# An encoder layer on one core: query norms moved into the softmax's exponential, and a bias table laid out backwards

## What is computed

```python
xn = rmsnorm(h, g_pre_mix)
proj = xn @ w_in                       # qa, ka, va, qb, kb, vb, gate_a, gate_b
qb = axial_rope(rmsnorm(qb.reshape(B, S, GQA_Q_HEADS, HEAD_DIM), g_q))    # 8 heads of 128
kb = axial_rope(rmsnorm(kb.reshape(B, S, GQA_KV_HEADS, HEAD_DIM), g_k))   # 2 heads
ya = neighbourhood_attention(qa, ka, va, rpb) @ w_branch_a                # bias from rpb, column mask
yb = gqa_attention(qb, kb, vb) @ w_branch_b
...
s = einsum(q, k) * Dh ** -0.5          # in both attentions
pr = softmax(s)
...
dc_idx = clip(kc - qc, -(NA_COLS - 1), NA_COLS - 1) + NA_COLS - 1
col_bias = rpb[:, :, dc_idx]           # bias of the neighbourhood attention
```

## Time and profile before

| | |
|---|---|
| Median of three runs (lowest, highest) | 2796.68 us (2796.5, 2797.44) |
| Span of the profiled execution | 2793.8 us |
| TensorE matmuls busy | 2759.9 us (99%) |
| VectorE, ScalarE, GpSimd busy | 1677.4, 997.8, 18.3 us |
| Mean granted TensorE clock | 0.998 |
| Attention stage, about | 323 to 812 us of the span |

### The profile page before, as it was taken

The page is one execution under the profiler, slowest core; times in us unless marked ns, Lnnn a source line. Parts: engine busy times, 40 slices in busy tenths (PEclk is TensorE's granted clock), DMA queues, the critical chain, the costliest instruction groups (busy, mean ns, idle before and its releaser), DMA issues.

```text
span 2793.8 us, 41330 instructions
## 1 busy us (share of the span) xinstructions
PE 2759.9 (99%) x16624; PEld 2465.9 (88%) x16624; DVE 1677.4 (60%) x2113; ACT 997.8 (36%) x1323; POOL 18.3 (1%) x25
## 2 busy tenths in 40 slices
PE   8999999999999999999999999999999999999997
PEld 7999888888888888878999999999998888888886
DVE  7888555555554432376888888888883233234534
ACT  7333323323334322253444444444442121113422
POOL 0000000000000000000000000000000000000000
PEclk9999999999999999999999999999999999999999
DMA  6434422222225444253433333333327352443322
GB/s 251 151 114 136 138 76 75 75 84 83 75 91 163 138 153 141 91 196 136 151 114 141 122 132 131 125 138 117 146 92 295 103 181 99 157 155 124 131 96 105
DMA packets 158298, 364.75 MB, mean 131 GB/s; under 512 B 17142, under 2 KB 51438, under 8 KB 155630
## 3 DMA queue, kind: packets, MB, share of 16 engines
q1 hardware_dynamic: 146304, 325.33, 34.1%
q10 hardware_dynamic: 11886, 37.87, 3.4%
HBM read 321.15 MB, written 42.00 MB: 130 GB/s over the span
## 4 chain that ended last, share of the span: by engine, by line
PE 87%; issue 10%; DVE 1%; ACT 1%; DMA 1%; SPq 0%; POOL 0%; DVEq 0%; POOLq 0%
PE bank L2204 10%; PE bank L2202 10%; PE bank L2203 10%; PE bank L2122 10%; PE bank L2124 10%; PE bank L2123 10%; PE bank L1948 8%; PE bank L1946 8%; PE bank L1947 8%; PE bank L1979 1%; DMA x_f<-xT 0%; DVE resid_b L1643 0%; PE bank L2271 0%; PE bank L1967 0%; ACT x_f L771 0%
## 5 line engine op out<-in xcount | busy, mean ns | idle before, releaser
L736 ACT CAST w_hi<-w_raw 128x1024 fp32r<-128x1024 f32 x290 | 292.3, 1052 | 934.6 <-PE bank L2204 522.7
L1188 DVE TENSOR_TENSOR w_lo<-w_raw,w_hi 128x1024 fp32r<-128x1024 f32 x288 | 341.0, 1222 | 454.4 <-ACT w_hi L736 454.3
L2122 PE MATMUL bank<-act_hi,w_hi 128*128 128x256 f32 x1664 | 471.2, 283 | 2.4 <-DVE act_lo L1279 1.4
L2123 PE MATMUL bank<-act_lo,w_hi 128*128 128x256 f32 x1664 | 470.9, 283 | 0.0
L2124 PE MATMUL bank<-act_hi,w_lo 128*128 128x256 f32 x1664 | 470.9, 283 | 0.0
L2122 PEld LDWEIGHTS bank<-act_hi,w_hi 128*128 128x128 f32 x1664 | 319.4, 192 | 2.9 <-DVE act_lo L1279 1.6
L2123 PEld LDWEIGHTS bank<-act_lo,w_hi 128*128 128x128 f32 x1664 | 319.5, 192 | 0.1
L2124 PEld LDWEIGHTS bank<-act_hi,w_lo 128*128 128x128 f32 x1664 | 319.5, 192 | 0.0
L1946 PE MATMUL bank<-act_hi,w_hi 128*128 128x512 f32 x752 | 299.5, 398 | 1.2 <-DVE w_lo L1188 1.2
L1947 PE MATMUL bank<-act_lo,w_hi 128*128 128x512 f32 x752 | 293.2, 390 | 0.0
L1948 PE MATMUL bank<-act_hi,w_lo 128*128 128x512 f32 x752 | 293.1, 390 | 0.0
(11 more groups left out here) (263 smaller groups left out, 5422.5 us busy)
## 6 DMA issues: line engine op xcount, KB each, us to landing
w_raw<-w_in SPq DMA_DIRECT2D x92, 512.0 KB, 4.2
w_raw<-w_ffn_out SPq DMA_DIRECT2D x88, 512.0 KB, 4.5
w_a_even<-w_ffn_in SPq DMA_DIRECT2D x80, 512.0 KB, 5.3
w_a_odd<-w_ffn_in SPq DMA_DIRECT2D x60, 512.0 KB, 4.4
hid_dram<-hid_st ACTq DMA_DIRECT2D x44, 512.0 KB, 5.2
w_raw<-w_ffn_in SPq DMA_DIRECT2D x36, 512.0 KB, 5.4
w_raw<-w_out SPq DMA_DIRECT2D x32, 512.0 KB, 4.5
w_raw<-w_ple_gate SPq DMA_DIRECT2D x32, 512.0 KB, 4.3
```

The source lines that it names most:

```text
L736: nc.scalar.copy(w_hi[:, 2 * par + half], w_raw[:, half]).then_inc(hi_ready, 1)
L1188: nc.vector.tensor_tensor(w_lo[:, 2 * par + half], w_raw[:, half], w_hi[:, 2 * par + half].bitcast(F32), ALU.subtract).then_inc(lo_ready, 1)
L2122: nc.tensor.matmul(out, w_hi[:, slot, k], hi, start=k == 0, stop=False)
L2123: nc.tensor.matmul(out, w_hi[:, slot, k], lo, start=False, stop=False)
```

## The change

**Norms.** For the query heads `diag`, the spread and the multiplication of `rope_c` are gone. The scores are formed with unscaled rotated queries, whose tokens are the rows of the score bank; so the token's factor is applied there: `rs` replaces the constant in the exponential's `scale` (one value per partition), and `neg_top` is `top * -1 * rs`. The mean square is taken with width 1 and epsilon `EPS * DH`, so `rs` holds the factor 128^-0.5 as well. The key heads keep their spread. **Table.** The host reverses the columns of `rpb`; the same 16 DMAs then land a table whose rows are in the right partitions and run backwards, and VectorE reads it from SBUF with a step of -1 while it adds the mask. `flip`, its DMA and the six matmuls are gone.

```diff
-        bias_flipped = at("bias_flipped", R_Q + 40 * KB, [P, HEADS, E_ROWS, GRID])
-        flip_t = at("flip_t", R_Q + 55 * KB, [P, P])
+        bias_back = at("bias_back", R_Q + 40 * KB, [P, HEADS, E_ROWS, GRID])
...
-            sp.dma_start(flip_t[:], flip).then_inc(mask_landed, 16)
...
                     ins = nc.scalar.activation(probs[:, t], src[:, t], ACT.Exp, bias=neg_top[:, which, t:t + 1],
-                                               scale=scale, accum_out=psum_p[:, which, t:t + 1])
+                                               scale=1.0 if scale is None else scale[:, t:t + 1],
+                                               accum_out=psum_p[:, which, t:t + 1])
...
-                exps(neg_top_b, hd + 1, scores, 0, SCALE, exp_b)
+                exps(neg_top_b, hd + 1, scores, 0, rs, exp_b)
...
-                nc.vector.tensor_scalar(var[:], bank[:, src_bank, 0:TT], 1.0 / width, EPS, ALU.mult,
+                nc.vector.tensor_scalar(var[:], bank[:, src_bank, 0:TT], 1.0 / width, EPS * DH / width, ALU.mult,
...
-                dve.wait_ge(mask_landed, 32)
+                dve.wait_ge(mask_landed, 16)
+                dve.wait_ge(table_landed, 16 * 2 * HEADS)
                 for i in range(first, end):
-                    dve.wait_ge(flipped, i + 1)
                     nc.vector.tensor_tensor(
                         bias[:].rearrange("p h e c -> p (h e) c")[:, 8 * i:8 * i + 8],
-                        bank[:, B_SCORE + i % 4].rearrange("p (a c) -> p a c", c=GRID),
+                        bias_back[:].rearrange("p h e c -> p (h e) c")[:, 8 * i:8 * i + 8, ::-1],
                         mask_t[:].unsqueeze(1).to_broadcast([P, 8, GRID]), ALU.add).then_inc(bias_read, 1)
...
-            def rope(e, q, g, hi, lo):
+            def rope(e, g, hi, lo, scaled_by=None):
...
-                diagonal(q)
+                if scaled_by is not None:
+                    diagonal(*scaled_by)
...
-                nc.vector.tensor_tensor(rope_c[:], rope_c[:], rope_s[:], ALU.add).then_inc(rope_added, 1)
-                dve.wait_ge(rope_added, e + 1)
-                dve.wait_ge(norm_spread, q + 1)
-                nc.vector.tensor_tensor(rope_c[:], rope_c[:], bank[:, B_NORM], ALU.mult).then_inc(rope_done, 1)
+                added = nc.vector.tensor_tensor(rope_c[:], rope_c[:], rope_s[:], ALU.add)
+                if scaled_by is None:
+                    added.then_inc(rope_done, 1)
...
-                mean_square(r + (e0 + 2), DH, B_NORM)
+                mean_square(r + (e0 + 2), 1, B_NORM)
...
-                nc.vector.tensor_scalar(neg_top[:, 0], top[:, 0], -SCALE, None, ALU.mult).then_inc(neg_top_b, 1)
+                dve.wait_ge(norm_root, r + (e0 + 3))
+                nc.vector.scalar_tensor_tensor(neg_top[:, 0], top[:, 0], -1.0, rs[:], ALU.mult,
+                                               ALU.mult).then_inc(neg_top_b, 1)
...
-                        pe.wait_ge(table_landed, 16 * 2 * HEADS)
-                        pe.wait_ge(mask_landed, 32)
-                        flip_bias(0, 4)
-                        pe.wait_ge(bias_read, 3)
...
-                    pe.wait_ge(bias_read, 4)
-                    flip_bias(4, BIAS_PARTS)
...
-                unit(n + 2, 0, tall(0), hooks={HALF: lambda: spread(r + (e0 + 2), B_NORM)})
+                unit(n + 2, 0, tall(0))
                 pe.wait_ge(rope_lo_ready, r + (e0 + 2))
-                if first and j == 0:
-                    pe.wait_ge(bias_read, BIAS_PARTS)
...
-        "rpb": lay(np.asarray(rpb)[0].reshape(-1, 2 * NA_COLS - 1)),
+        "rpb": lay(np.asarray(rpb)[0].reshape(-1, 2 * NA_COLS - 1)[:, ::-1]),
```

More of the change, by code:

```diff
@@ L69 @@
 NORM_FFN_IN = 1 + KV * (1 + PER_KV)
+SPREAD_FFN_IN = 1 + KV
 MIX, FFN, PLE_N = range(3)
@@ L151, in shape_constants @@
             rot[m - half // 2, m] = 1.0
-    flip = np.zeros((P, P), np.float32)
-    for m in range(P):
-        flip[(m // GRID) * GRID + GRID - 1 - m % GRID, m] = 1.0
     qc = np.arange(P)[:, None] % GRID
@@ L1196, in mean_square, with diagonal @@
                 dve.wait_ge(norm_summed, q)
-                nc.vector.tensor_scalar(var[:], bank[:, src_bank, 0:TT], 1.0 / width, EPS, ALU.mult,
+                nc.vector.tensor_scalar(var[:], bank[:, src_bank, 0:TT], 1.0 / width, EPS * DH / width, ALU.mult,
                                         ALU.add).then_inc(norm_var, 1)
-            def diagonal(q, first=False):
+            def diagonal(q, d):
                 dve.wait_ge(norm_root, q + 1)
-                if not first:
-                    dve.wait_ge(norm_spread, q)
+                if d:
+                    dve.wait_ge(norm_spread, d)
                 nc.vector.tensor_tensor(diag[:], ident_t[:].unsqueeze(1).to_broadcast([P, TT, P]),
@@ L1341, in _ @@
             dve.wait_ge(ident_landed, 16)
-            diagonal(0, True)
+            diagonal(0, 0)
             weight_sum(0, 0, 1, H_GATES)
@@ L1432, in rope @@
                 dve.wait_ge(rope_c_ready, e + 1)
-                nc.vector.tensor_tensor(rope_c[:], rope_c[:], rope_s[:], ALU.add).then_inc(rope_added, 1)
-                dve.wait_ge(rope_added, e + 1)
-                dve.wait_ge(norm_spread, q + 1)
-                nc.vector.tensor_tensor(rope_c[:], rope_c[:], bank[:, B_NORM], ALU.mult).then_inc(rope_done, 1)
+                added = nc.vector.tensor_tensor(rope_c[:], rope_c[:], rope_s[:], ALU.add)
+                if scaled_by is None:
+                    added.then_inc(rope_done, 1)
+                else:
+                    _, d = scaled_by
+                    added.then_inc(rope_added, 1)
+                    dve.wait_ge(rope_added, d)
+                    dve.wait_ge(norm_spread, d + 1)
+                    nc.vector.tensor_tensor(rope_c[:], rope_c[:], bank[:, B_NORM], ALU.mult).then_inc(rope_done, 1)
                 dve.wait_ge(rope_hi_ready, e + 1)
@@ L1497, in head @@
                 na_low(hd * 2 + 1, ka_hi, ka_lo)
-                mean_square(r + (e0 + 2), DH, B_NORM)
+                mean_square(r + (e0 + 2), 1, B_NORM)
                 if not first:
                     low_pT(pT_hi_a, hd + (-1), pT_lo_a)
-                rope(r + (e0 + 1), r + (e0 + 2), 0, q_hi, q_lo)
+                rope(r + (e0 + 1), 0, q_hi, q_lo)
                 dve.wait_ge(na_lo_ready, hd * 2 + 1)
@@ L1520, in head @@
                 dve.wait_ge(score_a, hd + 1)
+                if first and j == 0:
+                    dve.wait_ge(bias_read, BIAS_PARTS)
                 for g in range(GROUPS):
@@ L2011, in sum_and_rotate @@
                 nc.tensor.matmul(bank[:, B_MISC], rot_t[:], qk_lo[:], start=False, stop=True).then_inc(qk_rotated, 1)
-            def flip_bias(first, end):
-                flat = bias_flipped[:].rearrange("p h e c -> p (h e c)")
-                for i in range(first, end):
-                    nc.tensor.matmul(bank[:, B_SCORE + i % 4], flip_t[:], flat[:, i * T:(i + 1) * T], start=True,
-                                     stop=True).then_inc(flipped, 1)
             def turn_group_values(j):
@@ L2051, in head @@
                 if first:
-                    unit(n, 0, tall(0), hooks={HALF: lambda: spread(e0 + 1, B_NORM)} if j else
-                         {3: lambda: sum_and_rotate(e0), HALF + 4: lambda: spread(e0 + 1, B_NORM)})
+                    unit(n, 0, tall(0), hooks={HALF: lambda: spread(1 + j, B_NORM)} if j else
+                         {3: lambda: sum_and_rotate(e0), HALF + 4: lambda: spread(1 + j, B_NORM)})
                     if j:
@@ L2056, in head @@
                         values_a(last_hd)
-                    else:
-                        pe.wait_ge(table_landed, 16 * 2 * HEADS)
-                        pe.wait_ge(mask_landed, 32)
-                        flip_bias(0, 4)
-                        pe.wait_ge(bias_read, 3)
                     turn_group_values(j)
@@ L2328, in _ @@
             unit(N_FFN + 2, (N_FFN + 2) % 2, tall(IN_BANKS[2]), free=False,
-                 hooks={HALF: lambda: spread(NORM_FFN_IN, B_H_NORM)})
+                 hooks={HALF: lambda: spread(SPREAD_FFN_IN, B_H_NORM)})
             unit(N_FFN + 3, (N_FFN + 3) % 2, tall(IN_BANKS[3]), free=False, hooks=turning(0, (5, 8, 11, 14)))
```

15 lines of the change are left out of this document (7 added, 8 removed).

## The result

| | before | changed |
|---|---|---|
| Median of five runs | 2796.50 us (2795.83 to 2797.44) | 2779.78 us (2779.60 to 2780.32) |
| Span of the profiled execution | 2793.8 us | 2778.5 us |
| Mean granted TensorE clock | 0.998 | 0.998 |

The ratio is 0.9942, with a 95% interval of 0.993 to 0.9954: the change makes the kernel 16.7 us (0.6%) faster. Forecast were 2781.0 us and a range of 2779.7 to 2783.4 us; the measured median is inside it, 0.08 us above its low end.

What follows compares the result with a forecast made beforehand. TensorE's instruction list was taken to bound the kernel; 7.2 + 6.15 + 1.71 + 0.64 = 15.7 us off 2793.8 us gives 2778.1 us, with 2.9 us carried over 2781.0 us; range 2779.7 to 2783.4 us.

Steps and rivals of the forecast that it cites:

- TensorE's list sets the time: Attention stage: it lasts as long as TensorE's instructions, busy 467.00 of 467.00 us; everything behind moves forward as a block.
- Query spreads: Eight query-head spreads removed from TensorE's list, 0.90 us each between matmul starts: 7.2 us, bounds 6.9 to 8.2 us.
- First turns: First head: without four table turns and a wait for VectorE, the values' turns start 6.15 us sooner.
- last turns: First head: without the remaining table turns, the sums of squares start in their place, 1.71 us sooner.
- The inner split: The 6.15 us before the first head's values' turns: 3.6 us of matmul and 2.56 us of wait for VectorE.
- SyncE's queue: Stage start: without the `flip_t` fetch the first head's weights come 0.64 us sooner, shortening TensorE's 1.23 us wait; bounds 0 to 0.64.
- the wait for the key's `diag`: TensorE's third small wait in the attention stage, 0.2 us, claimed to stay because it hangs on the same fetch.
- The covers: Slack before TensorE waits: 3.3 us from `q_lo` to the first head's scores, 4.9 us from normalising to turning the probabilities.
- Backward reading: VectorE's six bias parts: no cost, hidden up to 1.85 us each; rival that it is dear, 2784.9 us at 2.5 us, chance 0.05.
- the scale per partition: ScalarE's exponentials: 0.08 us a pass, 0.3 us a head, hidden; rival that it makes the kernel slower, chance 0.02.
- From the span to the median: Whole kernel: the median stands 2.9 us above the profiled span, carried over to the changed kernel.

Runs made afterwards that it cites:

- that half alone: Kernel before with only the norms' part of the change, the table still turned by TensorE; 2788.40 us against 2796.03 us, ratio 0.9973.
- e9_other_banks: Kernel before with its first four table turns in banks 2, 3, 5 and 6 instead of 2 to 5; 2791.59 us, one execution, against 2795.81 us.
- e8_bias_x5: Changed kernel with four extra backward additions ahead of each bias part, into an unused buffer; 2790.20 us, span 2788.4 us.
- e7_bias_x2: Changed kernel with one extra backward addition ahead of each bias part, into an unused buffer; 2779.50 us, span 2777.7 us.
- e6_exps_x4: Changed kernel with three extra exponential passes ahead of each of a query head's four passes, into an unused buffer; 2807.03 us, span 2805.2 us.
- e5_exps_x2: Changed kernel with one extra exponential pass ahead of each of a query head's four passes, into an unused buffer; 2778.92 us, span 2777.1 us.

## Why the prediction was right, step by step

**TensorE's list sets the time.** Right. Busy 460.00 of 460.00 us in the stage, and the last head moved by as much as the span.

**Query spreads, 8 x 0.90 = 7.2 us.** Right: 0.91 us a head is 7.3 us, and the timing of that half alone gave 7.6 us. The price came from the starts of matmuls on both sides of a spread. The record's length, 1.02 us, would have said 8.2 us.

**First turns, 6.15 us; last turns, 1.71 us.** Right. From the old place of the turns the changed kernel is 344.26 - 337.92 = 6.34 us ahead, 0.19 us of which it already had at the end of unit `n` (338.11 against 337.92). The sums of squares are 357.39 - 349.29 = 8.10 us ahead, so the last turns gave 1.76 us. The inner split, 3.6 us of matmul and 2.56 us of wait, is 3.4 and 2.7 in `e9_other_banks`.

**SyncE's queue, 0.64 us.** Right in mechanism on the mean (the weights are issued 0.62 us sooner), too large in size, and wrong for the profiled execution, where the wait grew from 1.23 to 1.41 us. The sum had taken one execution's landing as the kernel's. It had also let the wait for the key's `diag` stay at 0.2 us; in seven profiles without the fetch it is none to 0.6 us and takes back part of the gain.

**The covers.** Right. `q_lo` is ready at 358.17 us and the scores start at 361.58, here as VectorE's and TensorE's timelines have them: 3.4 us, forecast 3.3. In the other heads the forecast had about 1.7 us more, 5.0 us, and the timelines show 4.2 us (4.6 us in the first head of the second group). The 0.53 us that VectorE waited for the root ahead of `diag` stand only in the first head, and the wait for the spread is shorter in the others; both had been taken off everywhere. It cost nothing, since 4.2 us is cover enough. Backward reading and the scale per partition cost 0 and 0.35 us, both hidden.

```profile
357.48 0.69 DVE L1440 TENSOR_TENSOR q_lo<-rope_c,q_hi 128x512 fp32r<-128x512 f32 x1 [0.69 <-ACT q_hi L876]
...
361.58 0.28 PE L1996 MATMUL bank<-k_hi,q_hi 128*128 128x256 f32 x1
```

On the Trainium skill's two rules: the backward read took what the forward one did, 686 ns for 512 columns, so the slower rates that "Vector Engine (DVE) Microarchitecture Reference" lists in "Measured stream behaviour on trn2" don't apply to a step of -1 in this shape (that a negative step was not measured stands in that page's section on performance modes, and not in the one that the forecast named); and the 93 ns per operand of "ScalarE: Activation LUTs", section "What ACT_TABLE_LOAD costs", agrees with the 87 ns here.

**From the span to the median.** This is the term that was mis-sized, by 1.1 us. I carried over 2.9 us between the profiled span and the median. An execution's own time is 1.8 us above its span: 2780.32 us goes with 2778.5. So the profiled execution before took about 2795.6 us and was a quick one beside runs from 2795.83 to 2797.44 us, while the changed kernel's profile is of its slowest run of five. With 1.8 us in place of 2.9 the forecast would have been 2779.9 us. By spans the sum was 0.4 us too large (15.3 against 15.7 us), by medians 1.0 us too small (16.7 against 15.7 us); both lie within the scatter of single executions. What the last microsecond between the terms measured (7.3 + 6.15 + 1.76 + about 0.4 to 0.5, so 15.7 us) and the medians' 16.7 us consists of is open: there is only one profile of the kernel before.

## What to carry to other kernels

When one engine's instruction list fills the time, price a removed instruction by the starts of its neighbours and not by its record, and then walk every producer to see which wait comes up next; the covers worked out in this way held to about 1 us even when they were spent on purpose. Work them out for a head that is not the first as well. A wait for a bank can be nearly as large as the matmuls around it (2.6 us against 3.6), and goes by choosing other banks. Before a stage, put the weights that are needed first ahead of tables that are needed 20 us later, and judge a DMA's landing from several executions.

## What the runs showed of the hardware

A wait of TensorE can cost more than itself. In `e8_bias_x5` the span is 10 to 11 us longer than in kernels like it (2777.7 us for `e7_bias_x2`) for a wait of 8.3 us. Busy time by stretch, with the granted clock third from the end: TensorE idles from 361 to 369 us, the clock falls from 1.00 to 0.50 (1.2 GHz of 2.4) during the idle time, and the twelve score matmuls and the first four of the next unit run slower until about 373.5 us. The score matmuls start 0.21 us apart there and 0.12 us apart in the changed kernel.

```profile
360.00:364.00 4.00, 1.11 (x5) 0.57 (x4) 3.90 (x6) 0.00 (x0) 0.00 (x0) 0.93 0.53 180
364.00:372.00 8.00, 2.56 (x12) 2.56 (x13) 7.25 (x12) 3.03 (x4) 1.01 (x1) 0.50 0.00 0
372.00:374.00 2.00, 2.00 (x7) 1.66 (x7) 1.81 (x4) 0.14 (x1) 0.00 (x0) 0.58 0.85 236
374.00:376.00 2.00, 2.00 (x10) 1.64 (x9) 0.43 (x1) 2.00 (x8) 0.00 (x0) 1.00 0.71 274
```

In `e6_exps_x4` waits of nearly one length had this effect in four heads of eight, the second, fourth, fifth and seventh, and not in the others; the longest wait, 2.85 us in the first head, kept 1.00. The second head, where the clock falls behind a wait of 2.27 us:

```profile
429.00:431.00 2.00, 0.55 (x3) 0.13 (x1) 0.56 (x3) 1.97 (x5) 0.00 (x0) 1.00 0.00 0
431.00:433.00 2.00, 1.18 (x9) 1.18 (x10) 2.00 (x5) 1.26 (x2) 0.00 (x0) 0.92 0.00 0
433.00:435.00 2.00, 2.00 (x12) 2.00 (x11) 1.63 (x2) 1.07 (x2) 0.00 (x0) 0.50 0.18 25
435.00:437.00 2.00, 2.00 (x9) 1.74 (x9) 1.25 (x4) 0.00 (x0) 0.00 (x0) 0.73 0.82 285
```

In the third head the wait is 2.27 us too, and each microsecond from 484 to 496 us shows 1.00. From the turning of the probabilities in one head to that in the next it is 56.97 us with such a fall between (431.82 to 488.79) and 55.43 us without (376.39 to 431.82). That is 1.5 us a fall and about 6 us for four. This kernel's span is 28.1 us over that of `e5_exps_x2`, 8.8 us more than its 19.3 us of waits, and these 6 us are the larger part of them. Most of the rest is there without a fall too: 55.43 us is 2.5 us over the changed kernel's 52.92 us, for a wait of 2.27 us. What decides whether a wait of this length brings the clock down, these runs do not show. The kernel before had a wait of 2.56 us for `bias` and kept 1.00 through it, so the change won nothing here beyond the wait.
